# The loads of the down weights move from SyncE's DMA ring to ScalarE's

## The chip, the cores and the metric

The kernel runs on one core of one Trainium2 chip. The metric is the device time of one execution in microseconds (us). Three executions of the kernel before took 2285.41, 2285.84 and 2285.99 us; the median is 2285.84 us. All tensors are float32 in HBM.

## The reference

One sequence of 256 tokens of width 1024 goes through two blocks. The first block has a modulation (`w_ada`), a mixer (retention and dilated attention) and a mixture of 16 experts. The second has two layers of feed-forward, a gated pooling and recurrence mixer, and feed-forward again. The change touches only the experts, so only they are shown:

```
def expert_choice_moe(h, w_router, w_gate, w_up, w_down):
    cap = EC_CAPACITY_FACTOR * S // E                        # 32 tokens for each of 16 experts
    affinity = jax.nn.softmax((h @ w_router).astype(jnp.float32), axis=-1)
    gates, idx = lax.top_k(jnp.swapaxes(affinity, 1, 2), cap)
    flat_idx = idx.reshape(B, E * cap)
    xe = h[b_idx, flat_idx].reshape(B, E, cap, D)
    a = jnp.einsum('becd,edf->becf', xe, w_gate)             # D = 1024, f = 2048
    u = jnp.einsum('becd,edf->becf', xe, w_up)
    ye = jnp.einsum('becf,efd->becd', jax.nn.silu(a) * u, w_down)
    ye = ye * gates[..., None].astype(ye.dtype)
    return jnp.zeros_like(h).at[b_idx, flat_idx].add(ye.reshape(B, E * cap, D))
```

Each expert has three weight matrices of 1024 x 2048 float32, 8 MB each, and each is read from HBM once. With 32 tokens an expert has little to compute, and much to load.

## The kernel before, in words

The kernel is written by hand for the five engines. Each engine has its own program, and they meet by semaphores only.

**The ring of slots.** Weights land in nine slots in SBUF, each of 4096 float32 per partition, which is 2 MB. A matrix of an expert is four such tiles: `("gate", q, j)`, `("up", q, j)`, `("down", q, j)` with q from 0 to 3. The order of consumption is gate 0 to 3, up 0 to 3, down 0 to 3, then the next expert, 192 tiles for the 16 experts. `expert_tiles` (L120) deals the tiles to the slots in that order, cyclically, so that a tile always takes the slot of the tile nine places earlier. The tile that stands nine places before down 0 of an expert is down 3 of the expert before it; for down 1, 2 and 3 it is gate 0, 1 and 2 of the same expert; for gate 0 of the next expert it is gate 3 of this one; for gate 1, 2 and 3 of the next it is up 0, 1 and 2 of this one; for up 0 it is up 3, and for up 1, 2 and 3 it is down 0, 1 and 2 of the expert before.

**Who loads.** SyncE (SP) issues every DMA of the program. In `load` (L609) it waits for `tile_done[s]`, the count of uses of slot s that TensorE has finished, and then issues one DMA of 2 MB, which raises `loaded[s]` by 16. Since SP works in program order, all tiles stand in one DMA queue in the order of their consumption. Expert 0 is loaded by straight code (`lead_tiles`, `turn` is None); experts 1 to 15 are five turns of a loop with three experts in each (L688).

**Who consumes.** TensorE (PE) runs `expert` (L1173) for each expert: it gathers the 32 tokens with one-hot products (L1178) in between the gate tiles, waits for `loaded` and multiplies each gate and up tile (L1198, 8 products), turns the gates' rows (L1185), turns the hidden activations (L1208), multiplies the down tiles (L1220) and adds the result to all tokens (L1241). After the last product on a tile it raises `tile_done`.

**ScalarE (ACT)** runs `expert` at L1699, four instructions for each expert: it copies the turned gates out of PSUM (L1701) once PE has done L1185, which PE issues right behind gate 3; it takes the SiLU (L1704), copies the turned hidden activations (L1706), and copies the result of the down products (L1709). Everything PE does next (L1241, then the next expert) waits for L1709.

**After the experts** SP waits for its slots with L715 and L716 and loads the tiles of the two layers (L745). The first layer tile takes the slot of the last expert's up 1, the second the slot of the last expert's down 3.

In this text T means the moment at which ACT starts L1701 of an expert, just after gate 3 of that expert is used; g, u and d with a number are its gate, up and down tiles.

Of the kernel before, what the change touches and what calls it, by code (L numbers as in the profile page):

```python
# [15 lines left out]
P = 128  # L16
D = 1024
# [13 lines left out]
FB = FF // 512  # L31
# [69 lines left out]
def first_tiles():  # L101


    order = [("ada", 0), ("ada", 1), ("ada", 2), ("ada", 3), ("win", 3), ("win", 4), ("ada", 4), ("ada", 5), ("win", 5),
             ("win", 0), ("ada", 6), ("win", 1), ("ada", 7), ("win", 2), ("ada", 8), ("wout", 0), ("ada", 9),
             ("wout", 1), ("ada", 10), ("ada", 11)]
    return [(name, 1, 0 if name[0] == "ada" else 2, first_slot(*name)) for i, name in enumerate(order)]
# [20 lines left out]
def layer_tiles():  # L128

    def ffn(f):  # L130
        up = [((kind, f, j), 1, 2) for j in range(5) for kind in ("upa", "upb")]
        return up + [(("upab", f), 2, 2)] + [(("dn", f, c), 1, 1) for c in range(KD)]

    mixer = [(("proj", i), 1, 2) for i in (1, 2, 3, 0)] + [("small", 3, 0)] + [(("proj", i), 1, 2) for i in range(4, 10)]
    mixer += [(("pup", 0), 1, 2)] + [(("lup", i), 1, 1) for i in range(4)] + [(("lout", i), 1, 2) for i in range(2)]
    tiles = ffn(0) + mixer + ffn(1)
    assert len(tiles) % SPLIT_SLOTS == 0
    return [(*tile, LAYER_SLOTS[i % SPLIT_SLOTS]) for i, tile in enumerate(tiles)]
# [146 lines left out]
def block_kernel(nc, a, out):  # L285

    def without_units(tiles):
        return [(name, dmas, slot) for name, dmas, _, slot in tiles]

    lead_tiles, turn_tiles = expert_tiles()  # L290
    ring_plan = Ring(without_units(first_tiles()), lead_tiles, turn_tiles, without_units(layer_tiles()))
# [6 lines left out]
    with ctx:  # L298
# [3 lines left out]
        def sem(name):  # L302
            return ctx.enter_context(nc.semaphore(name))
# [112 lines left out]
        y_part = yp_  # L416

        (u_, sa_, _) = carve((FK * S, 4 * 512, FK * S))
        u_lo, u_hi = work_r[:, 0:FK * S], work_r[:, FK * S + 4 * 512:2 * FK * S + 4 * 512]
        silu_a = sa_.rearrange("p (b n) -> p b n", b=4)  # L420
# [77 lines left out]
        loaded = [sem(f"loaded{s}") for s in range(SLOTS)]  # L498
        tile_done = [sem(f"tile_done{s}") for s in range(SLOTS)]
# [67 lines left out]
        def slot_view(name, k, n):  # L567

            s = ring_plan.slot(name)
            if s < SLOTS - OUTER_SLOTS:  # L570
                memory = ring[:, s, :]
            else:
                at = OUTER + (s - (SLOTS - OUTER_SLOTS)) * SLOT
                memory = work[:, at:at + SLOT]
            return memory[:, 0:k * n].rearrange("p (k n) -> p k n", k=k)
# [31 lines left out]
        def _(sp):  # L607
            def load(name, dst, src, turn=None):

                s = ring_plan.slot(name)  # L610
                if turn is None:
                    if ring_plan.before(name):
                        sp.wait_ge(tile_done[s], ring_plan.before(name))
                else:
                    sp.wait_ge(tile_done[s], ring_plan.before(name, turn))
                    sp.sem_inc(slot_granted, 1)
                sp.dma_start(dst, src).then_inc(loaded[s], 16)
# [30 lines left out]
            for name, _, _, _ in first_tiles()[4:]:  # L648
                kind, i = name
# [24 lines left out]
            def expert_weights(e, tiles, turn):  # L674

                gate = a["w_gate_e"][0][bass.ds(e, 1)].rearrange("a (p k) n -> p (a k) n", p=P)
                up = a["w_up_e"][0][bass.ds(e, 1)].rearrange("a (p k) n -> p (a k) n", p=P)
                down = a["w_down_e"][0][bass.ds(e, 1)].rearrange("a (q p b) n -> p (a q) b n", p=P, q=FB)
                for name, _, _ in tiles:
                    kind, q, _ = name  # L680
                    if kind == "down":
                        load(name, slot_view(name, 4, D), down[:, q], turn)
                    else:
                        w = gate if kind == "gate" else up
                        load(name, slot_view(name, 2, FF), w[:, 2 * q:2 * q + 2, :], turn)

            expert_weights(0, lead_tiles, None)
            with sp.Fori(0, TURNS) as turn:  # L688
                for j in range(TOGETHER):
                    expert_weights(turn * TOGETHER + (j + 1), turn_tiles[3 * FB * j:3 * FB * (j + 1)], turn)  # L690
# [5 lines left out]
            with sp.Fori(0, LAYERS) as l:  # L696
# [11 lines left out]
                for name, _, _, _ in layer_tiles():  # L708
# [9 lines left out]
                    kind = name[0] if isinstance(name, tuple) else name  # L718
# [29 lines left out]
            name = ("upa", 0, 0)  # L748
# [729 lines left out]
        def _(act):  # L1478
# [220 lines left out]
            def expert(e, j, turn):  # L1699
                act.wait_ge(gT_done, e + 1)  # L1700
                act.copy(gT_, bank[3][:, 0:S]).then_inc(gT_ready, 1)  # L1701
                name = ("gate", FB - 1, j)
                act.wait_ge(tile_done[ring_plan.slot(name)], ring_plan.done(name, turn))
                act.activation(silu_gate, bank[0], ACT.Silu).then_inc(silu_ready, 1)  # L1704
                act.wait_ge(hiddenT_done, e + 1)
                act.copy(hT_, bank[2]).then_inc(hiddenT_ready, 1)  # L1706
                name = ("down", FB - 1, j)
                act.wait_ge(tile_done[ring_plan.slot(name)], ring_plan.done(name, turn))
                act.copy(y_part, two_banks[1]).then_inc(y_ready, 1)  # L1709

            expert(0, 0, 0)
            with act.Fori(0, TURNS) as turn:
                for j in range(TOGETHER):
                    expert(turn * TOGETHER + (j + 1), j + 1, turn)
# [947 lines left out]
```

## Time and profile before

| | |
|---|---|
| median of three executions | 2285.84 us |
| the profiled execution, its own time | 2291.06 us |
| its span, first to last instruction | 2289.3 us |
| TensorE busy | 1956.7 us, 85% of the span |
| VectorE busy | 1051.6 us, 46% |
| ScalarE busy | 688.8 us, 30% |
| bytes moved by DMA | 658.17 MB |
| mean granted TensorE clock | 0.919 of full speed |

The profile comes from one execution. It lists when each instruction ran on each engine, what ended the engine's idle time before it, and how busy the sixteen DMA engines of the core were. The time outside the span is 1.8 us. The stage of the experts is the stretch from about 206 us to about 1122 us; before it lies the mixer of the first block, behind it the two layers.

### The profile page before, as it was taken

What the parts mean: (1) busy time and instruction counts of PE and PEld (TensorE: products, weight loads), DVE (VectorE), ACT (ScalarE), POOL (GpSimd) and SP (SyncE); (2) the same over time, 40 slices, a digit from 0 to 9 for tenths busy, and PEclk for the clock granted to TensorE, in tenths of its full rate; (3) what the DMA queues carried; (4) which work ended last, traced back from release to release, by engine and by line L of the source; (5) the groups of instructions that cost most, each with busy time, mean ns of one, the idle gap of its engine ahead of it and who ended that gap; (6) DMA issues with size and microseconds to landing.
All of it is one profiled execution on the core that took longest, in us unless ns stands there. A gap on an engine that the chain in (4) does not pass through costs nothing.

```text
span 2289.3 us, 30404 instructions
## 1 busy us (share of the span) xinstructions
PE 1956.7 (85%) x12514; PEld 1402.9 (61%) x12514; DVE 1051.6 (46%) x1247; ACT 688.8 (30%) x771; POOL 35.0 (2%) x25
## 2 busy tenths in 40 slices
PE   7998766676666666766799999999999999999999
PEld 6775222222222222222488899988888889998887
DVE  5753000000000000000387677877768767787776
ACT  3543000000000000000244448453444444845344
POOL 0100000000000000000000002000000000200000
PEclk9997788878888888788899999999999999999999
DMA  8787999999999999999854655555575565555554
GB/s 317 275 303 317 428 428 427 429 428 429 427 430 427 429 427 429 428 429 428 327 184 149 200 175 188 174 188 189 142 223 184 150 200 175 187 175 178 190 152 131
DMA packets 232943, 658.17 MB, mean 288 GB/s; under 512 B 6356, under 2 KB 121476, under 8 KB 208260
## 3 DMA queue, kind: packets, MB, share of 16 engines
q1 hardware_dynamic: 232836, 656.67, 74.9%
q8 instruction: 76, 1.25, 0.2%
q14 instruction: 31, 0.25, 0.0%
HBM read 655.60 MB, written 1.05 MB: 287 GB/s over the span
## 4 chain that ended last, share of the span: by engine, by line
issue 78%; PE 19%; DVE 1%; DMA 1%; POOL 1%; SPq 0%; ACT 0%; DVEq 0%; POOLq 0%; ACTq 0%
PE psum L1291 3%; PE psum L1292 2%; PE psum L1313 2%; PE psum L1314 2%; PE psum L1395 2%; PE psum L1315 2%; PE psum L1396 1%; DVE ring_r L2319 1%; PE psum L966 1%; PE psum L968 1%; PE psum L967 1%; PE psum L853 0%; DMA ring<-in_w_out_dram 0%; PE psum L1362 0%; DMA work<-in_pool_scale_dram 0%
## 5 line engine op out<-in xcount | busy, mean ns | idle before, releaser
L2319 DVE TENSOR_TENSOR ring_r<-ring,ring_r 128x2048 fp32r<-128x2048 f32 (+2 forms) x182 | 452.8, 2519 | 101.0 <-ACT ring_r L1726 100.3
L1291 PE MATMUL psum<-work_r,ring_r 128*128 128x512 f32 x1280 | 452.8, 399 | 5.2 <-DVE ring_r L2319 5.2
L1726 ACT CAST ring_r<-ring 128x2048 fp32r<-128x2048 f32 (+2 forms) x180 | 360.2, 2041 | 286.3 <-PE psum L1396 120.9
L1292 PE MATMUL psum<-work_r,ring_r 128*128 128x256 f32 x1280 | 359.5, 281 | 0.0
L1291 PEld LDWEIGHTS psum<-work_r,ring_r 128*128 128x128 f32 x1280 | 240.5, 188 | 66.2 <-issue 6.3
L1198 PE MATMUL psum<-ring,work 128*32 128x512 f32 x1280 | 193.8, 734 | 96.2 <-DMA ring<-in_w_up_e_dram 70.9
L1313 PE MATMUL psum<-work_r,ring_r 128*128 128x256 f32 x928 | 263.3, 284 | 2.5 <-DVE ring_r L2319 2.5
L1314 PE MATMUL psum<-work_r,ring_r 128*128 128x256 f32 x928 | 262.2, 283 | 0.0
L1315 PE MATMUL psum<-work_r,ring_r 128*128 128x256 f32 x928 | 261.9, 282 | 0.0
L1395 PE MATMUL psum<-work_r,ring_r 128*128 128x512 f32 x704 | 247.3, 396 | 2.7 <-DVE ring_r L2319 2.7
L1292 PEld LDWEIGHTS psum<-work_r,ring_r 128*128 128x128 f32 x1280 | 241.8, 189 | 0.0
L2295 DVE TENSOR_SCALAR work<-psum,wide_cols,mod 128x32 f32<-128x32 f32 x128 | 33.9, 306 | 442.3 <-PE psum L1178 442.3
L1396 PE MATMUL psum<-work_r,ring_r 128*128 128x256 f32 x704 | 197.0, 280 | 0.0
L2308 DVE TENSOR_TENSOR work<-work,psum 128x512 f32<-128x512 f32 x16 | 11.0, 687 | 397.1 <-PE psum L1198 397.1
L1220 PE MATMUL psum<-ring,work 128*32 128x512 f32 x752 | 129.7, 824 | 71.9 <-DMA ring<-in_w_down_e_dram 64.2
L1313 PEld LDWEIGHTS psum<-work_r,ring_r 128*128 128x128 f32 x928 | 177.2, 191 | 5.3 <-issue 4.0
L1314 PEld LDWEIGHTS psum<-work_r,ring_r 128*128 128x128 f32 x928 | 177.3, 191 | 0.1
L1315 PEld LDWEIGHTS psum<-work_r,ring_r 128*128 128x128 f32 x928 | 177.1, 191 | 0.0
L1198 PEld LDWEIGHTS psum<-ring,work 128*32 128x32 f32 x1280 | 39.2, 122 | 213.3 <-DMA ring<-in_w_up_e_dram 113.5
L1198 PE MATMUL psum<-work 128*32 128x512 f32 x768 | 119.6, 752 | 58.1 <-DMA work<-in_w_up_e_dram 48.0
L1395 PEld LDWEIGHTS psum<-work_r,ring_r 128*128 128x128 f32 x704 | 132.1, 188 | 35.4 <-issue 3.9
L2395 DVE TENSOR_REDUCE work<-psum 128x512 f32<-128x1024 f32 x88 | 107.1, 1221 | 75.2 <-PE psum L1292 71.4
(324 smaller groups left out, 2138.3 us busy)
## 6 DMA issues: line engine op xcount, KB each, us to landing
ring<-in_w_down_e_dram SPq DMA_DIRECT2D x47, 2048.0 KB, 40.4
ring<-in_w_gate_e_dram SPq DMA_DIRECT2D x42, 2048.0 KB, 40.4
ring<-in_ffn_w_up_dram SPq DMA_DIRECT2D x41, 2048.0 KB, 7.9
ring<-in_w_up_e_dram SPq DMA_DIRECT2D x38, 2048.0 KB, 40.5
work<-in_w_up_e_dram SPq DMA_DIRECT2D x26, 2048.0 KB, 40.5
ring<-in_w_in_dram SPq DMA_DIRECT2D x25, 2048.0 KB, 8.0
work<-in_w_gate_e_dram SPq DMA_DIRECT2D x22, 2048.0 KB, 40.8
ring<-in_ffn_w_down_dram SPq DMA_DIRECT2D x32, 1408.0 KB, 7.1
```

The source lines that it names most:

```text
L1198: mm = pe.matmul(dst[32 * g:32 * g + 32, :], xe[:, 2 * q + k, :], w[:, k, 512 * g:512 * (g + 1)], start=(q == 0 and k == 0), stop=(q == FB ...
L1220: mm = pe.matmul(two_banks[1][32 * b:32 * b + 32, 512 * half:512 * (half + 1)], hiddenT[:, b, 32 * q:32 * q + 32], w[:, b, 512 * half:512 ...
L1291: pe.matmul(dst, w_hi[:, k, cols], h_both(k), start=(k == 0), stop=False)
L1292: mm = pe.matmul(dst[:, 0:S], w_lo[:, k, cols], h_hi_[:, S * k:S * (k + 1)], start=False, stop=(k == KD - 1))
L1313: pe.matmul(out_b, w_hi[:, k, cols], hi[:, tokens], start=(k == 0), stop=False)
L1314: pe.matmul(out_b, w_hi[:, k, cols], lo[:, tokens], start=False, stop=False)
L1315: mm = pe.matmul(out_b, w_lo[:, k, cols], hi[:, tokens], start=False, stop=(k == n_k - 1))
L1395: pe.matmul(dst, w_hi[:, k, :], u_both(k), start=(k == 0), stop=False)
L1396: mm = pe.matmul(dst[:, 0:S], w_lo[:, k, :], u_hi[:, S * k:S * (k + 1)], start=False, stop=(k == FK - 1))
L1726: act.copy(hi_unit(name, unit), raw_unit(name, unit)).then_inc(hi_ready, 1)
L2319: dve.tensor_tensor(lo_unit(name, unit), raw_unit(name, unit), hi_unit(name, unit).bitcast(F32), ALU.subtract).then_inc(lo_ready, 1)
L2395: dve.tensor_reduce(dst.rearrange("p (c t) -> p c t", c=2), src, AX.X, ALU.add).then_inc(emptied["dve"], 1)
```

## The change

The twelve loads of an expert are divided between two engines. SP still issues the gate and up tiles, and all twelve of expert 0. The four down tiles of experts 1 to 15 are issued by ACT, on ScalarE's own DMA ring, each behind the same wait on `tile_done` as before. They stand in ACT's program behind the copy of the turned gates (L1701) and ahead of the SiLU. The count of slots, the dealing of tiles to slots, the sizes and the semaphores for landing are the same. SP's increments of `slot_granted` for these tiles go; nothing waits for that semaphore.

```diff
@@ expert_weights, SyncE @@
-                down = a["w_down_e"][0][bass.ds(e, 1)].rearrange("a (q p b) n -> p (a q) b n", p=P, q=FB)
                 for name, _, _ in tiles:
                     kind, q, _ = name
-                    if kind == "down":
-                        load(name, slot_view(name, 4, D), down[:, q], turn)
-                    else:
+                    if kind != "down":
                         w = gate if kind == "gate" else up
                         load(name, slot_view(name, 2, FF), w[:, 2 * q:2 * q + 2, :], turn)
+                    elif turn is None:
+                        down = a["w_down_e"][0][e].rearrange("(q p b) n -> p q b n", p=P, q=FB)
+                        load(name, slot_view(name, 4, D), down[:, q], turn)
@@ expert, ScalarE @@
                 act.wait_ge(gT_done, e + 1)
                 act.copy(gT_, bank[3][:, 0:S]).then_inc(gT_ready, 1)
+                down = a["w_down_e"][0][bass.ds(e, 1)].rearrange("a (q p b) n -> p (a q) b n", p=P, q=FB)
+                for q in range(FB if j else 0):
+                    name = ("down", q, j)
+                    act.wait_ge(tile_done[ring_plan.slot(name)], ring_plan.before(name, turn))
+                    act.dma_start(slot_view(name, 4, D), down[:, q]).then_inc(loaded[ring_plan.slot(name)], 16)
                 name = ("gate", FB - 1, j)
```

On SP, in the body of the loop over turns, the first expert of a turn ends with these rows before; `tile_done` with a number is the semaphore of that slot.

```order
L617 DMA work<-in_w_up_e_dram 128x4096 [waits tile_done6]
L617 DMA work<-in_w_up_e_dram 128x4096 [waits tile_done7]
L615 REGISTER_ALU
L617 DMA ring<-in_w_down_e_dram 128x4096 [waits tile_done2]
L617 ISA [waits tile_done3]
L617 DMA ring<-in_w_down_e_dram 128x4096
L617 ISA [waits tile_done8]
L617 DMA work<-in_w_down_e_dram 128x4096
L617 ISA [waits tile_done0]
L617 DMA ring<-in_w_down_e_dram 128x4096
L617 ISA [waits tile_done4]
L617 DMA ring<-in_w_gate_e_dram 128x4096
```

The same place on SP in the changed kernel:

```order
L617 DMA work<-in_w_up_e_dram 128x4096 [waits tile_done6]
L617 DMA work<-in_w_up_e_dram 128x4096 [waits tile_done7]
L617 ISA [waits tile_done4]
L617 DMA ring<-in_w_gate_e_dram 128x4096
L615 REGISTER_ALU
L617 ISA [waits tile_done1]
L617 DMA ring<-in_w_gate_e_dram 128x4096
```

The four down loads are gone, and the next expert's gate 0 stands right behind up 3.

On ACT, the first expert of the loop's body, before: the copy of the turned gates, the SiLU, the copy of the turned hidden activations and the copy of the result.

```order
L1701 COPY work<-psum 128x256 [waits gT_done]
L1703 ISA
L1704 ACTIVATE work<-psum 128x512 [waits tile_done4]
L1706 COPY work<-psum 128x512 [waits hiddenT_done]
L1708 REGISTER_ALU
L1709 COPY work<-psum 128x1024 [waits tile_done0]
```

The same place on ACT in the changed kernel, where line numbers behind the new code are higher by five:

```order
L1701 COPY work<-psum 128x256 [waits gT_done]
L1705 ISA
L1706 ISA [waits tile_done2]
L1706 DMA ring<-in_w_down_e_dram 128x4096
L1706 ISA [waits tile_done3]
L1706 DMA ring<-in_w_down_e_dram 128x4096
L1705 REGISTER_ALU
L1706 ISA [waits tile_done8]
L1706 DMA work<-in_w_down_e_dram 128x4096
L1706 ISA [waits tile_done0]
L1706 DMA ring<-in_w_down_e_dram 128x4096
L1709 ACTIVATE work<-psum 128x512 [waits tile_done4]
```

The four loads, with their waits, stand between the copy and the SiLU. The rows of PE are the same in both kernels.

## Rows read from the trace of the kernel before

**Rows 1.** The page: span, DMA share and rate in 40 slices, the queues.
```profile
span 2289.3 us, 30404 instructions
...
DMA  8787999999999999999854655555575565555554
GB/s 317 275 303 317 428 428 427 429 428 429 427 430 427 429 427 429 428 429 428 327 184 149 200 175 188 174 188 189 142 223 184 150 200 175 187 175 178 190 152 131
...
q1 hardware_dynamic: 232836, 656.67, 74.9%
q8 instruction: 76, 1.25, 0.2%
```

**Rows 2.** Windows: stretch, length, busy of PE, PEld, DVE, ACT, POOL, clock, DMA share, GB/s.
```profile
313.20:1077.10 763.90, 514.06 (x3198) 179.34 (x3198) 40.77 (x130) 32.13 (x53) 0.00 (x0) 0.82 1.01 428
254.00:294.00 40.00, 26.40 (x132) 4.97 (x132) 0.69 (x1) 1.40 (x4) 0.00 (x0) 0.66 1.00 426
...
610.00:620.00 10.00, 4.92 (x36) 0.82 (x32) 0.00 (x0) 0.00 (x0) 0.00 (x0) 0.76 1.02 436
```

**Rows 3.** Waits of PE from 313 to 1077 us: total, times, longest.
```profile
PE psum L1198 <- DMA ring<-in_w_up_e_dram: 60.8, 30, 3.0
PE psum L1220 <- DMA ring<-in_w_down_e_dram: 55.8, 30, 3.0
```

**Rows 4.** DMA issues by line: count, KB each, median us from issue to landing.
```profile
ring<-in_w_down_e_dram SPq DMA_DIRECT2D x47, 2048.0 KB, 40.4
...
out_dram<-work SPq DMA_DIRECT2D x2, 512.0 KB, 3.0
```

**Rows 5.** Timeline of ACT: start, length, instruction, and idle time before it.
```profile
253.88 0.37 ACT L1701 COPY work<-psum 128x256 f32<-128x256 f32 x1 [15.50 <-PE psum L1185]
...
313.23 0.37 ACT L1701 COPY work<-psum 128x256 f32<-128x256 f32 x1 [18.28 <-PE psum L1185]
...
1077.08 0.37 ACT L1701 COPY work<-psum 128x256 f32<-128x256 f32 x1 [17.77 <-PE psum L1185]
...
1117.40 1.01 ACT L1709 COPY work<-psum 128x1024 f32<-128x1024 f32 x1 [19.00 <-PE psum L1220]
```

**Rows 6.** Timeline of ACT, the result copy of expert 0.
```profile
237.37 1.01 ACT L1709 COPY work<-psum 128x1024 f32<-128x1024 f32 x1 [7.19 <-PE psum L1220]
```

**Rows 7.** Timeline of PE, up tiles of expert 1 (a tile is x16).
```profile
256.35 3.17 PE L1198 MATMUL psum<-ring,work 128*32 128x512 f32 x16 [2.51 <-DMA ring<-in_w_up_e_dram]
...
271.04 3.35 PE L1198 MATMUL psum<-work 128*32 128x512 f32 x16 [1.25 <-DMA work<-in_w_up_e_dram]
```

**Rows 8.** Timeline of PE, start of expert 0, start of expert 1, and down 3 of two experts.
```profile
206.40 3.62 PE L1178 MATMUL psum<-work 128*128 128x32 f32 x16 [1.62 <-DVE work L2281]
209.95 3.17 PE L1198 MATMUL psum<-work 128*32 128x512 f32 x16
...
242.00 1.87 PE L1178 MATMUL psum<-work 128*128 x16
243.79 1.92 PE L1198 MATMUL psum<-ring,work 128*32 128x512 f32 x16
...
643.74 1.92 PE L1220 MATMUL psum<-ring,work 128*32 128x512 f32 x16 [1.53 <-DMA ring<-in_w_down_e_dram]
...
1113.82 3.50 PE L1220 MATMUL psum<-ring,work 128*32 128x512 f32 x16 [2.97 <-DMA ring<-in_w_down_e_dram]
```

**Rows 9.** Timeline of SP, four issues in a row that wait for nothing.
```profile
3.12 2.07 SPq L643 DMA_DIRECT2D ring<-in_w_ada_dram  x4
```

**Rows 10.** Timeline behind the last expert, all engines.
```profile
1119.11 2.36 DVE L2327 CAST ring_r<-ring 128x2048 fp32r<-128x2048 f32 x2 [22.21 <-DMA ring<-in_ffn_w_up_dram]
...
1134.17 0.40 PE L1362 MATMUL psum<-work_r,ring_r 128*128 128x512 f32 x1
```

## The prediction

> **What bounds the kernel now.** I read the page's forty slices first. From slice 5 to slice 19 the DMA engines are busy all the time and move 428 GB/s, and behind that the rate falls to about 180 [rows 1]. So the kernel has a stage that is bound by transfers, and it is the experts'. The windows confirm it for thirteen whole experts: from 313.2 to 1077.1 us the DMA share is 1.01 and the rate is 428 GB/s [rows 2]. Those 13 experts are 156 tiles in 763.9 us, so one tile takes L = 4.90 us and an expert of 12 tiles 58.8 us. The waits of PE say the same from the other side: nearly every tile makes PE wait for its landing, up to 3.0 us each [rows 3]. The issue table shows how deep the queue is: a tile lands 40.4 us after its issue, though its own transfer is worth 4.90 us [rows 4], so some eight tiles stand in line. That line is what keeps the DMA engines at work through every pause of PE. In this stage only two things can move the time: bytes per second, and a DMA engine without work.
>
> **What the change takes away.** Sixty loads leave SP's program. SP was never late (the line is eight tiles deep), so this gives nothing. The 60 increments of `slot_granted` and some register work go with it, also at nothing.
>
> **What it adds on ACT.** Four waits and four issues for each of 15 experts, between the copy L1701 and the SiLU. The waits are for down 3 of the expert before and for gates 0, 1 and 2, all used before the copy can start, so they pass at once. SP's four issues in a row take 2.07 us [rows 9]; ACT's then delay the SiLU by about 2 us. The product that needs the SiLU comes after up 3, over ten us later by the up tiles' landings [rows 7]. That cover holds even if PE runs the four up tiles without a wait, at 1.92 us each. Cost: nothing.
>
> **What it moves.** Two things, and the second is the dear one. First, the down tiles are now asked for only at T, not as each slot comes free. Second, they no longer stand in the one line. From T on there are two lines, and something must divide the DMA engines between them. No row of before shows two long lines at once, so I bound it. At the one end ACT's line gets everything until it is empty, and its four tiles take 4 L = 19.6 us. At the other end it gets what SP's line leaves: SP can hold at most five ready tiles at that point (gates 0 to 3 and up 0 of the next expert, since up 1 waits for this expert's down 0), and the four down tiles are in after 9 L = 44.1 us. I take equal parts: all tiles are alike in size, each line has work all through, and the four tiles then take 8 L = 39.2 us. The only nearby rows are those of the instruction queue, q8, whose 76 packets went through beside q1 [rows 1] without any engine waiting out q1's 40 us line; that speaks for turns and against strict order of arrival, but they are few and small.
>
> The Trainium skill, page "DMA: Bandwidth & Descriptors", section "Queues, rings and completion order", says that each DMA engine goes round-robin between the rings that have work, a packet at a time. With equal tiles that is the 8 L of my middle case; no run here shows it yet.
>
> **The new chain.** With the parts equal, a loop closes through PE that did not bind before: T, issue, landing of down 3, PE's use of it, the copy L1709, the next expert's gather and gate tiles, the next T. Its steps:
> - copy and first issue: 0.37 us [rows 5] and about 0.3 us more, 0.7 us;
> - start and completion of a transfer into an empty line: a store of 512 KB lands after 3.0 us [rows 4], of which 1.2 us are its bytes at 428 GB/s, so 1.8 us;
> - four tiles at half rate: 39.2 us;
> - down 3 on PE up to L1709: 1.92 us where the granted clock is full (at 643.74) [rows 8] and 3.50 us where part of it is at the lower of the two levels (1113.82), with 0.1 us to the copy. PE will have idled some 6 us before it, longer than the 3 us pauses of now, and in the stretch from 254 to 294, with one tile each 4.90 us, the clock is 0.66 [rows 2]. I take 3.6 us;
> - from L1709 to the next T with every gate tile in place: 237.37 to 253.88 [rows 6, 5], 16.5 us. Here PE waited for no gate tile. The gates will be in place in the new order too: SP's line is not held up by down tiles.
>
> The sum is 61.8 us for each expert, against 58.8 us that the transfers need. From the T of expert 1 to the T of expert 15 are 14 such rounds: 865.2 us, where the trace of before has 1077.08 - 253.88 = 823.2 us [rows 5]. That is +42.0 us.
>
> At first this costs no DMA time. At T of expert 1 the last up tile is still 271.04 - 254.6 = 16.4 us away [rows 7, 5], 3.4 tiles of stock in SP's line. Each round eats 3.0 us of it. After five or six experts the up tiles are all in at T, and the DMA engines stand idle for about 3 us an expert, from the end of SP's ready tiles to T plus the start-up. The stock is given back at the end: after the last T there are no further gates, only one layer tile shares with the four down tiles, and T to L1709 becomes 0.7 + 1.8 + 5 x 4.90 + 3.6 = 30.6 us instead of 1117.40 - 1077.08 = 40.3 us [rows 5]. That is -9.7 us. Behind it nothing changes: PE's first layer product at 1134.17 comes after the norm of the experts' sum, and the split of the first layer tile, whose earlier landing the new order brings (it starts at 1119.11), is done before that [rows 10], so an earlier landing gives nothing.
>
> In total +32.3 us. The sum is made against the profiled execution: 2291.06 + 32.3 = 2323.4 us. That execution lies 5.2 us over the median of the runs, so the time to expect is 2285.84 + 32.3 = 2318 us.
>
> **Bounds inside this case.** With the clock full at down 3 a round is 60.2 us: 842.8 - 823.2 = +19.6, and -11.3 at the end, +8 us (2294). If the gather and the first gate tile run at the lower level too, as at the start of expert 0 (3.62 against 1.87 us and 3.17 against 1.92 us) [rows 8], a round is 64.8 us: +84 - 9.7, +74 us (2360). One microsecond in the round is 14 in the result, so this range is wide by its nature.
>
> **Rivals.**
> - *No change.* Two ways lead to it. ACT's issues may be served in the order of arrival with SP's (or end up in the same queue q1, so that the change does not do what it says), or ACT's line may get clearly more than half. Then down 3 lands after the stock of up tiles, one gate and the four down tiles; as the stock falls this shortens, the loop closes in less than 58.8 us, and the transfers bind again. For it: 428 GB/s is reached already, and the bytes are the same. Against it: the q8 packets. Price: between 0 and one tile, since the layer tile may go ahead of the last down tile: 2286 to 2291 us.
> - *Faster.* A second line could fill small gaps at the end of each transfer. Over 168 tiles, going from 428 GB/s to the 436 of one stretch of 10 us [rows 2] would take 0.09 us from each, 15 us in all: 2271 us. It decides only if ACT's line gets so much that the loop closes in under 58 us, that is, four down tiles within some 35 us of their issue. Against it: the DMA share is already 1.00 to 1.01 [rows 2], so there are no gaps to fill.
> - *ACT's line starves.* SP's ready tiles go first. The four down tiles take 44.1 us, a round 66.7 us: +110.6 - 9.7, 2387 us. Nothing in the rows speaks for it but SP's head start.
>
> The Trainium skill, same page, section "Issuing engines are not separate DMA queues", says that transfers issued by several engines run on the same sixteen DMA engines and interleave, and that issuing from several only saves time on the issuing engine. Read as a rule on time, it gives the first rival, no change; the trace of before agrees that there is no rate to gain.
>
> **Chances.** Equal parts with the loop binding: 0.70. No change: 0.16. Faster: 0.07. Starved: 0.07. The predicted time is that of the first, 2318 us. The range reaches down to 2284, which takes in the case of no change, and up to 2352, which leaves out the coldest rounds and the starved line. A measurement of this kernel can tell a difference from about 0.2%, 4.6 us. Faster by more than that: 0.07. Within it: 0.16. Slower by more: 0.77.
>
> **What would show it.** A second hardware queue with about 126 MB. From T on, down tiles that land some 9.8 us apart, and up tiles in the first experts too. A median from issue to landing of about 26 us for the down tiles, since the first lands after 11.6 and the last after 41 us. T to T of about 62 us. A DMA share near 1.00 for the first five or six experts and of about 0.95, 407 GB/s, behind them. PE waiting up to 8 us for a down tile. What would make it wrong: down tiles 4.9 us apart behind T, a share of 1.00 up to the last expert, or L1709 to T far from 16.5 us.

## The result, and the profile after

The changed kernel takes 2361.12 us (median of four runs, 2357.85 to 2365.77), the kernel before beside it 2285.62 us. The ratio is 1.0327, with a 95% interval of 1.0303 to 1.0351: slower by 75 us. Run again on another chip it was 1.0333 (1.0302 to 1.0363), and from the fifth T on its rounds from T to T take 64.9 us on average, as in the first run. The forecast was slower, 2318 us, with a range up to 2352. Direction and mechanism held, the size did not.

The page of the changed kernel: span, DMA share and rate in 40 slices, and the queues. These answer to [rows 1].

```profile
span 2364.0 us, 30371 instructions
...
DMA  8787999989999999999965564464565556545554
GB/s 315 268 337 309 427 429 427 404 380 382 387 384 422 388 386 381 384 386 381 380 222 180 147 218 168 150 235 165 159 194 183 182 157 213 183 153 205 178 157 129
...
q1 hardware_dynamic: 224196, 530.84, 60.0%
q10 hardware_dynamic: 8640, 125.83, 12.5%
```

There is a second hardware queue, q10, with the 125.83 MB of the 60 down tiles. The expert stage now fills the slices up to the twentieth, each 59.1 us long, and from slice 9 on the rate is mostly 380 to 388 GB/s instead of 428. The windows of the stage (columns as in [rows 2]) say how the loss sets in:

```profile
254.00:320.00 66.00, 41.54 (x268) 14.69 (x264) 3.14 (x10) 2.94 (x5) 0.00 (x0) 0.77 1.01 427
320.00:380.00 60.00, 34.41 (x208) 12.69 (x212) 3.14 (x10) 2.19 (x3) 0.00 (x0) 0.74 1.01 428
380.00:500.00 120.00, 66.51 (x413) 22.29 (x406) 3.82 (x11) 5.13 (x8) 0.00 (x0) 0.74 0.98 417
500.00:700.00 200.00, 122.79 (x780) 48.89 (x778) 10.46 (x34) 7.70 (x12) 0.00 (x0) 0.74 0.92 388
```

At first the two lines together move exactly what one line moved, 427 and 428 GB/s at a share of 1.01. A second ring costs no rate and gives none. Then the stock of up tiles (those still on their way at T) is eaten, and the DMA engines go idle for a part of every round. Here is that part in one round, in finer windows:

```profile
695.00:700.00 5.00, 5.00 (x40) 3.34 (x39) 1.06 (x4) 0.00 (x0) 0.00 (x0) 1.00 1.00 426
700.00:705.00 5.00, 5.00 (x48) 2.76 (x48) 1.39 (x5) 0.00 (x0) 0.00 (x0) 1.00 0.49 206
705.00:708.00 3.00, 3.00 (x30) 0.88 (x26) 0.00 (x0) 0.09 (x1) 0.00 (x0) 1.00 0.00 0
708.00:710.00 2.00, 2.00 (x24) 0.54 (x20) 0.00 (x0) 0.29 (x1) 0.00 (x0) 1.00 0.69 188
```

The share is 0.49 in 700 to 705 and 0.00 in 705 to 708: about 6 us without work, which end only when ScalarE's and SyncE's next issues take hold behind T. ACT's timeline shows the same round from T to T (ACTq is the issuing of a DMA):

```profile
707.91 0.37 ACT L1701 COPY work<-psum 128x256 f32<-128x256 f32 x1 [16.79 <-PE psum L1185]
708.05 1.97 ACTq L1706 DMA_DIRECT2D ring<-in_w_down_e_dram  x4
710.13 0.60 ACT L1709 ACTIVATE work<-psum 128x512 f32<-128x512 f32 x1 [1.84 <-issue]
...
754.77 1.01 ACT L1714 COPY work<-psum 128x1024 f32<-128x1024 f32 x1 [37.64 <-PE psum L1220]
772.67 0.37 ACT L1701 COPY work<-psum 128x256 f32<-128x256 f32 x1 [16.89 <-PE psum L1185]
```

And PE's, from the end of the up tiles to the addition of the result:

```profile
712.98 1.90 PE L1198 MATMUL psum<-work 128*32 128x512 f32 x16
715.78 0.72 PE L1208 MATMUL psum<-ident,work 128*128 128x128 f32 x4 [0.90 <-DVE work L2313]
721.78 3.59 PE L1220 MATMUL psum<-ring,work 128*32 128x512 f32 x16 [5.28 <-DMA ring<-in_w_down_e_dram]
731.48 3.64 PE L1220 MATMUL psum<-ring,work 128*32 128x512 f32 x16 [6.11 <-DMA ring<-in_w_down_e_dram]
741.27 3.64 PE L1220 MATMUL psum<-ring,work 128*32 128x512 f32 x16 [6.15 <-DMA ring<-in_w_down_e_dram]
751.06 3.64 PE L1220 MATMUL psum<-ring,work 128*32 128x512 f32 x16 [6.15 <-DMA ring<-in_w_down_e_dram]
755.83 5.43 PE L1241 MATMUL psum<-work 128*128 128x256 f32 x16 [1.13 <-ACT work L1714]
```

The reader is to see the starts of the four down tiles: 9.70, 9.79 and 9.79 us apart, twice the 4.90 us of the kernel before. That is the equal division. The SiLU starts 2.2 us behind T and is needed at 715, so the issues on ScalarE are indeed covered.

### The profile page after: what moved, and what is told of

Same layout as the page of the kernel before. It is cut to its first block, busy times and chain, and to the rows that moved or that the text cites. A ratio compares the mean times of both kernels' runs of the same rounds, so it can differ in the third digit from the quotient of the medians.

```text
span 2364.0 us, 30371 instructions
## 1 busy us (share of the span) xinstructions
PE 1942.1 (82%) x12514; PEld 1420.9 (60%) x12514; DVE 1051.5 (44%) x1247; ACT 690.1 (29%) x771; POOL 35.0 (1%) x25
## 3 DMA queue, kind: packets, MB, share of 16 engines
q10 hardware_dynamic: 8640, 125.83, 12.5%
## 4 chain that ended last, share of the span: by engine, by line
issue 78%; PE 18%; DVE 1%; DMA 1%; POOL 1%; SPq 0%; ACT 0%; DVEq 0%; POOLq 0%; ACTq 0%
PE psum L1291 3%; PE psum L1292 2%; PE psum L1313 2%; PE psum L1314 2%; PE psum L1395 2%; PE psum L1315 2%; PE psum L1396 1%; DVE ring_r L2324 1%; PE psum L966 1%; PE psum L968 0%; PE psum L967 0%; PE psum L853 0%; PE psum L1362 0%; SPq L635 0%; DMA ring<-in_w_out_dram 0%
## 5 line engine op out<-in xcount | busy, mean ns | idle before, releaser
L1220 PE MATMUL psum<-ring,work 128*32 128x512 f32 x752 | 158.3, 990 | 226.3 <-DMA ring<-in_w_down_e_dram 222.9
L1291 PEld LDWEIGHTS psum<-work_r,ring_r 128*128 128x128 f32 x1280 | 240.9, 188 | 64.0 <-issue 5.5
L1292 PEld LDWEIGHTS psum<-work_r,ring_r 128*128 128x128 f32 x1280 | 242.5, 189 | 0.0
L1220 PEld LDWEIGHTS psum<-ring,work 128*32 128x32 f32 x752 | 27.9, 153 | 335.2 <-DMA ring<-in_w_down_e_dram 233.9
L1313 PEld LDWEIGHTS psum<-work_r,ring_r 128*128 128x128 f32 x928 | 177.2, 191 | 5.2 <-issue 4.0
L1314 PEld LDWEIGHTS psum<-work_r,ring_r 128*128 128x128 f32 x928 | 177.3, 191 | 0.1
L1315 PEld LDWEIGHTS psum<-work_r,ring_r 128*128 128x128 f32 x928 | 177.1, 191 | 0.0
L1198 PE MATMUL psum<-ring,work 128*32 128x512 f32 x1280 | 152.6, 613 | 18.4 <-DMA ring<-in_w_up_e_dram 18.4
L1714 ACT COPY work<-psum 128x1024 f32<-128x1024 f32 x16 | 16.2, 1012 | 509.7 <-PE psum L1220 509.7
L1395 PEld LDWEIGHTS psum<-work_r,ring_r 128*128 128x128 f32 x704 | 131.9, 187 | 34.5 <-issue 4.0
L1396 PEld LDWEIGHTS psum<-work_r,ring_r 128*128 128x128 f32 x704 | 132.8, 189 | 0.0
```

The lines of the kernel that those rows point to most:

```text
L1198: mm = pe.matmul(dst[32 * g:32 * g + 32, :], xe[:, 2 * q + k, :], w[:, k, 512 * g:512 * (g + 1)], start=(q == 0 and k == 0), stop=(q == FB ...
L1220: mm = pe.matmul(two_banks[1][32 * b:32 * b + 32, 512 * half:512 * (half + 1)], hiddenT[:, b, 32 * q:32 * q + 32], w[:, b, 512 * half:512 ...
L1291: pe.matmul(dst, w_hi[:, k, cols], h_both(k), start=(k == 0), stop=False)
L1292: mm = pe.matmul(dst[:, 0:S], w_lo[:, k, cols], h_hi_[:, S * k:S * (k + 1)], start=False, stop=(k == KD - 1))
L1313: pe.matmul(out_b, w_hi[:, k, cols], hi[:, tokens], start=(k == 0), stop=False)
L1314: pe.matmul(out_b, w_hi[:, k, cols], lo[:, tokens], start=False, stop=False)
```

## The account of the 75 us

Between the two profiled spans lie 2364.0 - 2289.3 = 74.7 us. The first T moved by 254.75 - 253.88 = 0.9. From there to the T of expert 15 the changed kernel takes 1161.81 - 254.75 = 907.1 us where the one before took 823.2 [rows 5]: +83.9. From that T to the result copy it takes 1190.72 - 1161.81 = 28.9 instead of 40.3: -11.4. Behind the copy it takes 1.4 us more. The sum is 74.8.

```profile
254.75 0.37 ACT L1701 COPY work<-psum 128x256 f32<-128x256 f32 x1 [15.18 <-PE psum L1185]
...
1161.81 0.37 ACT L1701 COPY work<-psum 128x256 f32<-128x256 f32 x1 [16.86 <-PE psum L1185]
...
1190.72 1.01 ACT L1714 COPY work<-psum 128x1024 f32<-128x1024 f32 x1 [19.71 <-PE psum L1220]
```

So all of it is in the 14 rounds, and each step of a round can be laid beside the forecast:

| step of the round | forecast, us | 707.91 to 772.67, us |
|---|---|---|
| T to the first issue | 0.7 | 0.14 |
| start and completion (from the first issue to PE's use of down 0, less 9.8) | 1.8 | 3.9 |
| four tiles at half rate | 39.2 | 39.1 |
| down 3 to the result copy | 3.6 | 3.7 |
| result copy to the next T | 16.5 | 17.9 |
| sum | 61.8 | 64.8 |

## The experiments

Each was timed beside the kernel before on its own chip, so ratios are compared, and not medians. Microseconds for a whole run are the ratio's part of 2286 us, unless another base is given. The loop over q on ScalarE, which issues the down loads, is called the issue loop; `...` stands for code left out.

**Asking early on ScalarE's ring.** Is it the closed round, or the second ring as such?

```diff
+                down = ...
+                for q in range(FB if j else 0):        # the issue loop, moved up
+                    ...
                 act.wait_ge(gT_done, e + 1)
                 act.copy(gT_, bank[3][:, 0:S]).then_inc(gT_ready, 1)
-                down = ...
-                for q in range(FB if j else 0):
-                    ...
```

> Edit: on ScalarE the four down loads of experts 1 to 15 move from behind the copy of the turned gates to ahead of its wait, so that each is asked for as soon as its slot comes free (down 0 right behind the result copy of the expert before, down 1 to 3 as gates 0 to 2 are used). Two rings as in the changed kernel. Theory A (the round T, issue, four tiles at half rate, down 3, result copy, gathers and gates, T is what costs; it took 64.8 us where the transfers need 58.8): the four down tiles now overlap the gates, the round falls to about 39.2 + 3.9 + 3.7 = 47 us from result copy to result copy, under 58.8, the DMA engines never run dry, and the time returns to that of the kernel before plus at most one tile: 2286 to 2292 us. Theory B (the second ring itself costs, by issue work on ScalarE or a slower start of each of its 60 transfers, 75 us / 60 = 1.26 us each): no change from 2361 us.

Measured: ratio 1.0037 (1.0021 to 1.0052), +8 us of 75. The 60 transfers are still on q10 with the same bytes, but the rate of the stage is whole again:

```profile
GB/s 314 275 324 309 428 428 428 428 428 428 428 428 428 428 428 428 428 428 428 276 148 164 185 209 183 156 193 183 150 231 159 166 184 200 183 165 183 185 161 131
```

Theory B would have kept the 75 us and falls. The 8 us that stay were more than the 0 to 5 expected, and the end of the stage in this run explains them:

```profile
1113.50 3.64 PE L1198 MATMUL psum<-ring,work 128*32 128x512 f32 x16 [5.21 <-DMA ring<-in_w_up_e_dram]
...
1119.82 3.64 PE L1220 MATMUL psum<-ring,work 128*32 128x512 f32 x16 [0.68 <-ACT work L1711]
...
1127.56 1.89 PE L1220 MATMUL psum<-ring,work 128*32 128x512 f32 x16
1129.53 1.01 ACT L1714 COPY work<-psum 128x1024 f32<-128x1024 f32 x1 [9.76 <-PE psum L1220]
```

The last tile that PE waits for comes at 1113.50, as in the kernel before (1113.82 [rows 8]), but it is up 3. The down tiles had overtaken it, so the hidden activations and all four down tiles are still to come: 16.0 us to the result copy instead of 3.6.

**Down 0 in SyncE's line.** Does one tile less at half rate open the round?

```diff
-                for q in range(FB if j else 0):
+                for q in range(1, FB if j else 0):
@@ SyncE, expert_weights @@
+                    elif q == 0:
+                        down = ...
+                        load(name, slot_view(name, 4, D), down[:, q], turn)
```

> Edit: the changed kernel, but down 0 of each expert stays with SyncE, in its old place in the line; ScalarE issues down 1 to 3. Theory A: three tiles at half rate are 29.4 us instead of 39.2, the round falls from 64.8 to 55.0 us, under the 58.8 us of the transfers, so the DMA engines have no idle time and the time is 2286 to 2294 us. Theory B (each transfer from ScalarE costs 1.26 us): 45 of 60 transfers are left, 2361 - 19 = 2342 us.

Measured: ratio 1.0026 (1.0010 to 1.0043), +6 us, and the whole rate in every slice of the stage:

```profile
GB/s 314 276 312 306 428 427 427 428 429 429 427 428 428 429 427 428 429 428 428 310 158 170 183 196 184 166 184 184 154 231 166 164 185 193 184 166 184 187 160 131
```

Theory A. Taking a quarter of the tiles off the ring took away nine tenths of the loss, as it must where a sum of 64.8 us has to fall under 58.8.

**Asking late in one line.** Is late asking the cost, or the second line?

```diff
                     if kind == "down":
+                        if turn is not None and q == 0:
+                            last_gate = ("gate", FB - 1, name[2])
+                            sp.wait_ge(tile_done[ring_plan.slot(last_gate)], ring_plan.done(last_gate, turn))
+                            sp.sem_inc(slot_granted, 1)
                         load(name, slot_view(name, 4, D), down[:, q], turn)
```

> Edit: the kernel before (all loads on SyncE's ring), but SyncE asks for the down tiles of experts 1 to 15 only when gate 3 of that expert is used, as late as the changed kernel does. Theory A (late asking alone is harmless, since the down tiles only have to pass the stock of up tiles in one line at full rate, 4.9 us each; the division of the DMA engines is what makes them late): down 3 lands after the stock of up tiles and four down tiles, the line is never empty, 2284 to 2290 us. Theory C (asking late is the cost, whichever the ring): about 2340 to 2361 us, with DMA share under 0.95.

Measured: 0.9984 (0.9970 to 0.9998). The down tiles are indeed asked for late, for they land 26.3 us after their issue instead of 40.4 [rows 4]:

```profile
ring<-in_w_down_e_dram SPq DMA_DIRECT2D x47, 2048.0 KB, 26.3
```

Late asking alone costs nothing. Since the interval lay just under 1, it was run once more in more rounds:

> The run with one ring and late asking once more, in more rounds, because its ratio of 0.9984 (0.9970 to 0.9998) would make it faster than both kernels. Expectation: nothing in the chain is shorter than in the kernel before (the line is full at 428 GB/s either way, and down 3 lands last), so the ratio is 1.000, with an interval that holds 1. If it is again 0.998 with an interval under 1, late asking gains something of its own.

Measured: 0.9992 (0.9983 to 1.0002). It is the kernel before within what can be told. If there is a gain, it is under 0.2%, and nothing in the chain accounts for one.

**A later issue.** In a closed round each microsecond counts 14 times.

```diff
+                if j:
+                    act.wait_ge(tile_done[ring_plan.slot(("up", 0, j))], ring_plan.done(("up", 0, j), turn))
                 for q in range(FB if j else 0):
```

> Edit: the changed kernel, but ScalarE also waits until up 0 of the expert is used before it issues the four down loads, some 1.7 us later than now where the up tiles are in place (up 0 runs from T to T + 1.8 us), and 3 to 4 us later in the first expert. Theory A (a closed round, in which each microsecond counts 14 times): about 1.7 x 14 plus 2, +26 us, 2387 us. Theory B (the cost is per transfer, and not in a chain): the issues have more than 10 us of cover before the first down tile is used, so 2361 us.

Measured: ratio 1.0390 (1.0373 to 1.0407), where the changed kernel has 1.0327 and 1.0333. That is 13 to 14 us more, and not 26 more. Neither number was right. The first three rounds did grow, to 70.3, 68.4 and 68.3 us, but from the fourth on a round takes 64.8 to 65.0 us, as without the wait. What gave the 1.9 us back is seen on PE in the same place of a round, the addition of the result behind down 3:

```profile
774.66 3.72 PE L1241 MATMUL psum<-work 128*128 128x256 f32 x16 [1.14 <-ACT work L1716]
```

It takes 3.72 us, the time at the full granted clock of 2.4 GHz, where the changed kernel has 5.43 us with a part of it at the lower level of 1.2 GHz, as the clock of 0.53 in its window around that place shows:

```profile
750.00:760.00 10.00, 7.81 (x27) 4.02 (x28) 0.00 (x0) 1.01 (x1) 0.00 (x0) 0.53 0.99 419
```

PE had idled 6.15 us before down 3 there, and 6.57 us before the one at 770.07 us here. The whole round agrees. From the fourth T on, T to the result copy takes 48.6 to 48.9 us here, where the changed kernel has 46.2 to 47.6, and the copy to the next T takes 16.2 us instead of 17.7 to 18.3. When the clock rises again behind such a pause is thus a part of the round, and it can hide a shift of 2 us. Why it rises earlier here is not shown by any run.

**A much later issue.** The same edit with up 3 in place of up 0: a shift several times larger than what the clock gave back.

> Edit: the changed kernel, but ScalarE waits until up 3 of the expert is used before it issues the four down loads, about 6.9 us later than now where the up tiles are in place. A wait for up 0, 1.9 us later, had left the round at 64.8 us, since down 3 and the products behind it then ran at the full granted clock (L1241 3.72 us instead of 5.43). Theory A (closed round): the clock can give back at most about 1.8 us of 6.9, so the round is 70 to 72 us; the first expert, whose up tiles are still on their way, adds some 20 us once; in all 2361 + 20 + 13 x (5.1 to 6.9) = 2447 to 2471 us. Theory B (cost per transfer, not a chain): the down tiles are used well behind, 2361 to 2380 us.

Measured: ratio 1.0834 (1.0813 to 1.0855). From the changed kernel's 1.0333 that is 0.0501 of 2288.5 us, +115 us; against 2361 us it makes 2476 us, 5 us over the expected interval. One round, from T to the result copy:

```profile
841.51 0.37 ACT L1701 COPY work<-psum 128x256 f32<-128x256 f32 x1 [16.68 <-PE psum L1185]
...
848.67 0.37 ACTq L1708 DMA_DIRECT2D ring<-in_w_down_e_dram  x1
...
895.68 1.01 ACT L1716 COPY work<-psum 128x1024 f32<-128x1024 f32 x1 [41.76 <-PE psum L1220]
```

The issue comes 7.16 us behind T and the round from 841.51 to the next T at 911.88 is 70.4 us; over the last ten rounds the mean is (1271.37 - 554.68) / 10 = 71.7 us, within the 70 to 72 expected. The round is closed, and what is put into it beyond the clock's play comes out in every expert.

**SyncE's next gates behind ScalarE's issues.** What are the 3.8 us of start and completion?

```diff
                         load(name, slot_view(name, 2, FF), w[:, 2 * q:2 * q + 2, :], turn)
+                        if turn is not None and kind == "up" and q == FB - 1:
+                            used = ("up", 0, name[2])
+                            sp.wait_ge(tile_done[ring_plan.slot(used)], ring_plan.done(used, turn))
+                            sp.sem_inc(slot_granted, 1)
```

> Edit: the changed kernel, but SyncE, behind up 3 of each expert, also waits until up 0 of that expert is used (T + 1.8 us where the up tiles are in place) before it asks for gate 0 of the next expert. ScalarE's first issue at T + 0.14 us is then ahead of SyncE's, where now SyncE's is 0.25 us ahead. In the changed kernel the first down tile lands 13.6 us after its issue, 9.8 of them for its bytes at half rate, 3.8 for start and completion. Theory S1 (3.8 us is what a 2 MB transfer from ScalarE's ring always takes to start and complete): SyncE's bytes start about as late as ScalarE's, nothing changes in the chain, 2361 us. Theory S2 (2 of the 3.8 us are waiting behind SyncE's issues for one generator of descriptors): each round is 2 us shorter, 2333 us, and the first down tile lands about 11 us after its issue.

Measured: ratio 1.0147 (1.0123 to 1.0170), more than half of the loss gone, although SyncE asks later. Both theories are missed: S1 had 2361 us, S2 2333, and this is 2319 by the ratio. The mean round from the fourth T on is (1126.34 - 449.77) / 11 = 61.5 us. Below is the time from issue to landing for the first down tile of the round at 818.45 us:

```profile
DMA to landing us min/median/max: 10.5/10.5/10.5
```

It was 13.6 us in the changed kernel, for the tile issued at 708.05. That is the 3 us. In the run with the wait the first three experts, whose last up tile is still on its way at T, have 14.4, 14.0 and 13.7 us; from the fourth to the fourteenth it is 9.1 to 10.8. But the reason given in S2, waiting for SyncE's issues at the generator, does not fit the other runs. In the run with up 3 the first down tile was issued 7 us after SyncE's first gate, whose transfers ran all that time, and took 13.9 us:

```profile
DMA to landing us min/median/max: 13.9/27.7/41.6
```

(min, median and maximum of the four tiles issued from 848.67 us on). The first down tile took 13.9 us in the run with early issues too, issued at 715.17. So it does not matter how long ago the other ring issued. What matters is which ring's line starts first, and it holds for SyncE's ring as well. In the changed kernel SyncE's next gate was issued at 707.80, only 0.25 us ahead of the first down tile, and it landed after

```profile
DMA to landing us min/median/max: 10.2/10.2/10.2
```

In this run SyncE's first gate is the one that comes second, 2.0 us behind, and it took 14.2 us. Between two rings, then, the first tile of the first line takes about 10 us and the first tile of the second about 14. The head start in time is not what counts, for 0.25 us gave as much as 2.0 us. That the DMA engines have already taken in some of the first line's work would explain it, but no run shows that directly. In the last expert of the changed kernel SyncE's next load is issued only at 1165.71, 3.8 us behind ScalarE's first, and the first down tile lands after 8.2 us.

**SyncE held until down 0 is used.** The same edit with `("down", 0, name[2])`.

> Edit: as the one before, but SyncE holds gate 0 of the next expert (and so all that stands behind it) until down 0 of this expert is used. It asks for the same bytes later. Theory A (the equal division of the DMA engines between two lines is what makes the down tiles late): the first down tiles now come at full rate, 4.9 us each, down 3 about 33 us after T instead of 43, the round T to T closes in about 55 us, under the 58.8 us of the transfers, the DMA engines have work all the time again and the time falls to 2286 to 2294 us although SyncE asks later. Rival D (what costs is that requests come late, so that the DMA engines run dry): holding SyncE back some 12 us in each round adds idle time, over 2361 us.

Measured: ratio 1.0299 (1.0273 to 1.0324), where 1.000 to 1.004 was expected. My reckoning of this run was wrong. I had followed it with the up tiles all in at T. With the down tiles no longer late, the DMA engines do not run dry before T, so up tiles are still on their way at T and share with the down tiles. Down 0 is then used only when up 3 has come. By then ScalarE's line is all but empty too: its last tile, issued at 828.67, is in by 862.0, since no tile of the four took more than 33.3 us. The first two rows are up 2 and up 3, which now come 9.79 us apart, so that the equal division strikes the up tiles:

```profile
844.24 3.64 PE L1202 MATMUL psum<-work 128*32 128x512 f32 x16 [6.16 <-DMA work<-in_w_up_e_dram]
854.03 3.34 PE L1202 MATMUL psum<-work 128*32 128x512 f32 x16 [6.15 <-DMA work<-in_w_up_e_dram]
...
855.00:860.00 5.00, 3.34 (x24) 0.99 (x20) 0.69 (x1) 0.59 (x1) 0.00 (x0) 0.81 1.02 433
860.00:865.00 5.00, 5.00 (x36) 1.42 (x32) 0.00 (x0) 0.00 (x0) 0.00 (x0) 0.66 0.41 125
```

The dry stretch moved from before T to behind down 0, at a share of 0.41 in these 5 us, and the mean round from the fourth T on is 62.5 us. This run doesn't separate A from D. Two others speak against D: asking late in one line costs nothing, and SyncE asking 1.8 us later in two lines made the kernel faster. What this run shows is that the round is again longer than 58.8 us while the DMA engines stand idle in another part of it.

**Two early tiles on ScalarE, two in SyncE's line.** Is the rest of 8 us the order of the last landings?

```diff
-                for q in range(FB if j else 0):        # early, ahead of the copy
+                for q in range(2 if j else 0):
@@ SyncE, expert_weights @@
+                    elif q >= 2:
+                        down = ...
+                        load(name, slot_view(name, 4, D), down[:, q], turn)
```

> Edit: the run with early issues on ScalarE, but only down 0 and 1 of experts 1 to 15 are on ScalarE's ring; down 2 and 3 stay in SyncE's line in their old places. With all four early the DMA engines were never idle and the last expert tile landed at 1113.5 us as in the kernel before (1113.8), but it was up 3, with the hidden activations and four down tiles still to come on TensorE: 16.0 us from there to the result copy, against 3.6 us before. Theory A (the 8 us left over are this order of the last landings and nothing else): down 3 is again the last to land, the result copy of expert 15 starts 3.6 us behind it, within 1 us of 1117.4, and the ratio to the kernel before is 0.998 to 1.001. Theory B (the second ring costs something for each of its tiles): half of the excess stays, a ratio of about 1.002.

Measured: ratio 1.0002 (0.9990 to 1.0013), with half of the tiles still on the second ring. The result copy of expert 15 starts at 1118.60 us, 1.2 us behind that of the kernel before. In one detail it was otherwise than expected: PE waited last for up 3, and down 3 was in place when PE came to it.

```profile
1105.57 3.59 PE L1201 MATMUL psum<-ring,work 128*32 128x512 f32 x16 [2.97 <-DMA ring<-in_w_up_e_dram]
...
1116.64 1.90 PE L1223 MATMUL psum<-ring,work 128*32 128x512 f32 x16
```

The interval leaves 1.002 out, so the second ring has no price per tile that can be seen.

## Why the prediction was right and wrong

**What bounds the kernel: right.** The expert stage is bound by bytes per second and by idle DMA time, and beyond that only by what PE has left to do when the last tiles are in. The edits that brought the rate back to 428 GB/s, with four, three or two of an expert's down tiles still on the second ring, brought the time back to 1.0037, 1.0026 and 1.0002.

**Nothing saved on SP, nothing paid on ACT: right.** The issues delay the SiLU by 1.8 us, and nothing waits for it.

**Equal parts between the two lines: right,** 39.1 against 39.2 us. Only the first tiles of the two lines are not alike: 10.2 us from issue to landing for SyncE's, 13.6 us for ScalarE's. The rule of the Trainium skill, page "DMA: Bandwidth & Descriptors", section "Queues, rings and completion order", to take turns between the rings, agrees with the trace: equal tiles from two rings land 9.79 us apart instead of 4.90. What the Trainium skill says on the same page, section "Issuing engines are not separate DMA queues", that such transfers interleave on the same DMA engines, is right for the rate (427 GB/s with both lines at work), but a reader who takes from it that the issuing engine doesn't matter would have been wrong by 75 us here. Interleaving keeps the sum of bytes and changes who gets them first.

**Start and completion: this step failed.** I took 1.8 us from a store of 512 KB [rows 4]; it was 3.8 to 3.9 us. The page of the kernel before had a better row: a load of 2048 KB into a line that is often empty lands after 7.9 us, and less 4.90 us for its bytes that is 3.0 us. The trace of the changed kernel agrees: the last expert's first down tile, with little beside it, took 8.2 us, 3.3 over 4.90. The rest comes with the second place, since SyncE's gate is issued 0.2 to 0.3 us ahead of the first down tile in every round from the fifth T on. The term stands in 14 rounds: 2.1 x 14 = 29 us.

```profile
ring<-in_ffn_w_up_dram SPq DMA_DIRECT2D x41, 2048.0 KB, 7.9
```

**From the result copy to T: mis-sized by 1.4 us.** I had priced the lower clock for down 3 and only in the bound for what follows. It was paid in L1241, 5.43 against 3.72 us: 20 us in all. T to the first issue was shorter than I took, 0.14 against 0.7 us, -8 us. These three make 2.9 us a round, 41 of the 43 us by which 2361 lies over 2318.

**The stock: right in kind, quicker in fact.** With up to 6.2 us lost per round instead of 3.0 the 16.4 us were gone at the fourth T, and not after five or six experts. Behind that the DMA share was 0.92 and the rate 388 GB/s, where 0.95 and 407 were forecast. At the end -11.4 us came back, where -9.7 was forecast. That this came out so near is partly luck, since the start-up in it was mis-sized too, and SyncE asked for the layer tile only 3.9 us behind T.

**The range** ended at 2352 us though the bound worked out inside the likeliest case was 2360 us. The round, 64.8 us, came out exactly at that bound, but by other terms, which is chance: the bound had put 3.0 us on the gathers and the first gate tile, and these ran at the full clock. Where a term is multiplied by 14, the range has to reach to the bound of the round.

**The rivals.** No change, faster, and the starved line did not come about: the rate did not rise, and the parts were equal.

## What to carry to other kernels

A transfer-bound stage lives on one long line in the order of use. Moving a part of the loads to a second ring leaves the rate as it is, but halves the speed of what is needed next in favour of what is needed later; if the loads are also asked for late, a round closes through the consumer, and each microsecond of it counts once per iteration, but for what the clock gives back. So add up the round (ask, start, bytes at the shared rate, use, next ask) and compare it with the bytes of an iteration at the full rate before splitting a queue. If it must be split, ask as early as the slots allow, and see to it that the tile with the least work behind it still lands last.

## What the hardware showed that was not expected

- Where two rings began at nearly the same time, the place of a line's first 2 MB tile decided 3 us. The ring that was second landed it 12.9 to 14.3 us after its issue in the changed kernel (rounds 2 to 14), and 13.8 to 14.1 us with the other ring issued 7 us before. Issued first, it landed after 9.1 to 10.8 us. The 9.8 us of its bytes at half rate are in the first two numbers.
- Behind the first tile, two rings with tiles of the same size shared the DMA engines evenly: the tiles of one came 9.70 to 9.79 us apart, against 4.90 with one ring, at the same total rate as one.
- PE's pause of 6 us before down 3 put the products behind it partly at the lower clock, 5.43 instead of 3.72 us for L1241. With the issue 1.9 us later they were at the full clock, and the round was just as long as before. A small shift inside a round can thus vanish, and a test of such a round needs a shift several times larger.
